# Expert gathers of two slots for 64 tokens, with the weighted sums in pairs on the two column halves of TensorE

## The reference

```python
q = (xb @ p['peer_wq']).reshape(PEER_CHUNK, PEER_HEADS, 2, PEER_KEY_HALF)
s = jnp.einsum('thcd,ckd->thck', q, p['peer_subkeys'])
sv, si = lax.top_k(s, PEER_TOPK)
...
gate = jax.nn.softmax(top_s, axis=-1)
u = jnp.take(p['peer_u'], eidx, axis=0)
v = jnp.take(p['peer_v'], eidx, axis=0)
act = jax.nn.gelu(jnp.einsum('ted,td->te', u, xb), approximate=False) * gate
return jnp.einsum('te,ted->td', act, v)
```

## Time and profile before

| what | value |
|---|---|
| times of 3 runs | 2964.49, 2954.89, 2937.0 us; median 2954.89 us |
| the profiled execution | 2938.93 us, of which the span from the first to the last instruction is 2936.8 us |
| mean granted TensorE clock | 0.88 of full speed |
| moved by DMA | 976.17 MB, of it 805.36 MB by the gathers |

### The profile page before, as it was taken

One profiled execution on the slowest core, in us unless ns is written; L12 is line 12 of the kernel. 1 busy time (PEld: TensorE's weight loads), 2 busy tenths in 40 slices (PEclk: granted clock), 3 DMA queues, 4 the chain that ended last, 5 costly groups with the idle time before them and its releaser, 6 DMA issues.

```text
span 2936.8 us, 25913 instructions
## 1 busy us (share of the span) xinstructions
PE 2216.8 (75%) x6672; PEld 1099.9 (37%) x6672; DVE 1858.5 (63%) x4486; ACT 1074.9 (37%) x2975; POOL 951.4 (32%) x868
## 2 busy tenths in 40 slices
PE   6997777769788878767768877777766787766765
PEld 1434433544444435323323323233453343432322
DVE  0134966884567758877865555453579575867775
ACT  2022444452345544333342233232235344433332
POOL 0001323333233323334343434330023333344553
PEclk8998888889898999888889989888988888888888
DMA  5455989988787799899999999995189879999997
GB/s 187 125 175 194 392 324 346 374 338 326 300 313 281 281 369 386 338 417 382 393 404 411 393 394 397 401 396 179 65 318 378 334 302 352 400 370 411 420 411 316
DMA packets 223768, 976.17 MB, mean 332 GB/s; under 512 B 18300, under 2 KB 71064, under 8 KB 125336
## 3 DMA queue, kind: packets, MB, share of 16 engines
q0 software_dynamic: 110592, 805.36, 68.2%
q1 hardware_dynamic: 113048, 169.32, 17.0%
HBM read 973.56 MB, written 1.05 MB: 332 GB/s over the span
## 4 chain that ended last, share of the span: by engine, by line
PE 36%; DMA 25%; DVE 22%; issue 9%; ACT 5%; POOL 2%; POOLq 0%; SPq 0%; DVEq 0%; ACTq 0%; PEldq 0%
DMA EXPERT<-in_peer_uv,FIX 21%; PE VS L853 13%; PE PA L722 10%; DVE EXPERT L1429 7%; PE PB L676 4%; DVE SCR L1081 3%; PE PB L842 2%; DVE ACC L1439 2%; DMA WT<-in_w_ada 2%; PE PA L750 2%; POOL EXPERT L598 2%; PE PB L790 1%; DMA WT<-in_w_in 1%; PE PA L798 1%; PE PA L738 1%
## 5 line engine op out<-in xcount | busy, mean ns | idle before, releaser
L853 PE MATMUL VS<-EXPERT,DIAG 128*128 128x512 f32 x2304 | 1137.2, 644 | 281.7 <-ACT DIAG L1036 271.2
L1429 DVE CUSTOM_DVE_ANT_0 EXPERT<-EXPERT,H 128x1024 f32<-128x1024 f32 x768 | 925.6, 1223 | 493.2 <-DMA EXPERT<-in_peer_uv,FIX 486.6
L598 POOL DMA_INDIRECT EXPERT<-in_peer_uv,FIX x768 | 900.0, 1172 | 988.0 <-PE VS L853 494.7
L853 PEld LDWEIGHTS VS<-EXPERT,DIAG 128*128 128x128 f32 x2304 | 458.0, 207 | 915.0 <-issue 532.0
L1029 ACT ACTIVATE GEL<-DOT 128x1 f32<-128x1 f32 x768 | 154.8, 202 | 1049.0 <-DVE DOT L1429 1047.5
L722 PE MATMUL PA<-WT,HT 128*128 128x512 f32 (+2 forms) x768 | 329.5, 584 | 51.0 <-ACT QTD L966 17.3
L590 POOL COPY FIX<-IDX 128x8 uint32 (+1 forms) x96 | 51.2, 533 | 966.8 <-PE VS L853 529.6
L1036 ACT ACTIVATE DIAG<-IDN,WEI 128x128 f32<-128x128 f32 x576 | 231.3, 402 | 126.1 <-PE VS L853 109.8
L1439 DVE SCALAR_TENSOR_TENSOR ACC<-EXPERT,WEI,ACC 128x1024 f32<-128x1024 f32 x192 | 245.9, 1281 | 2.2 <-ACT WEI L1031 1.8
L842 PE MATMUL PB<-HT,WT 128*128 128x128 f32 (+1 forms) x1280 | 200.5, 322 | 46.6 <-issue 46.6
L1031 ACT ACTIVATE WEI<-GEL,GATE 128x1 f32<-128x1 f32 x768 | 226.2, 295 | 24.9
(11 more groups left out here) (137 smaller groups left out, 1656.5 us busy)
## 6 DMA issues: line engine op xcount, KB each, us to landing
WT<-in_w_ada SPq DMA_DIRECT2D x96, 512.0 KB, 7.1
WT<-in_peer_wq SPq DMA_DIRECT2D x80, 512.0 KB, 9.4
WT<-in_w_in SPq DMA_DIRECT2D x56, 512.0 KB, 10.5
WT<-in_w_out SPq DMA_DIRECT2D x40, 512.0 KB, 4.8
EXPERT<-in_peer_uv,FIX POOLq DMA_INDIRECT x768, 10.5
WT<-in_w_in SPq DMA_DIRECT2D x16, 384.0 KB, 7.2
WT<-in_w_in SPq DMA_DIRECT2D x20, 288.0 KB, 6.8
WT<-in_mla_wk_up SPq DMA_DIRECT2D x5, 512.0 KB, 3.9
```

What stands on the lines that cost most here:

```text
L598: pool.indirect_dma_start(out=EXPERT[:, j, :], out_offset=None, in_=a["peer_uv"], in_offset=bass.IndirectOffsetOnAxis(ap=FIX[:, par, j:j + ...
L853: ins = nc.tensor.matmul(VSUM[n][:, :], DIAG[:, i, :], EXPERT[:, j, D + n * W:D + (n + 1) * W], start=first, stop=last_one)
L1429: nc.vector.tensor_tensor_reduce(out=EXPERT[:, j, 0:D], in0=EXPERT[:, j, 0:D], in1=H2[:, b % HB, :], scale=1.0, scalar=0.0, op0=ALU.mult, ...
```

## The change

A gather now brings, in one buffer of EXPERT, two slots for 64 tokens in place of one slot for 128: buffers with an even number carry tokens 0 to 63, with an odd number tokens 64 to 127, and in each the lower 64 partitions hold one slot of these tokens and the upper 64 partitions the next one. The bytes and the number of gathers are the same. What follows from it:

- `apply` on PE works on a pair of buffers. The stationary matrix of each is 128x64 (two scaled 64x64 identities on top of each other, TWO times WEI), so that the product sums the two slots and gives 64 output rows: those of the even buffer go to partitions 0 to 63 of VS0 and VS1, those of the odd one to partitions 64 to 127, which are the two column halves of the array. A pair has four products (eight MATMULs), a quad eight products (sixteen MATMULs) in place of six (twelve). PE does all slots; DVE's `apply` and the clearing of ACC are gone.
- DIAG is 128x64 with eight buffers (one for each of EXPERT's), made for every slot; it no longer waits for PE.
- POOL waits for PE alone.
- IDX and GATE are written with slots and tokens rearranged: four instructions of 64 partitions x 8 elements for each, IDX's on DVE, GATE's on ACT, which now waits for DVE's reciprocal. That reciprocal is moved ahead of the comparison with IOTA.
- H2 holds each half of the tokens twice (`back`: eight copies of 64x512 for a block in place of two of 128x512) and has two buffers in place of three; IDX and GATE keep three (`IB`). `back` of the second latent block of layer 0 is moved behind the search for that block and the modulation beside it.
- ACC shrinks to 512 columns, MROW moves into unused partitions of QTM, and `close` is rewritten: the gate's row is copied first, and multiplied with the bank.

```diff
-HB = 3
+HB = 2
+IB = 3
+G = P // 2
-BY_PE = 3
...
-        out += [("norm", l, g, t, 2), ("back", l, g, t)]
+        out += [("norm", l, g, t, 2)] + ([("back", l, g, t)] if t == ts[0] else [])
...
+    if s[0] in ("pick", "also") and s[3] == 1:
+        return [("close", b - IB) for b in blocks_of(s[1], s[2]) if b >= IB]
...
-    picks = mingle(picks[5:], modulation(1, 0, 4)) + [("mod", 1, 1)]
+    picks = mingle(picks[5:], modulation(1, 0, 4)) + [("mod", 1, 1), ("back", 0, LAT, 1)]
...
-        H2 = sb("H2", [P, HB, D])
+        H2 = sb("H2", [P, HB, 2, D])
-        DIAG = sb("DIAG", [P, BY_PE, P])
+        TWO = sb("TWO", [P, G])
+        DIAG = sb("DIAG", [P, RING, G])
...
-                    if j % 4 < BY_PE:
-                        wait(used_pe, (n * 2 - 2 + j // 4) * BY_PE + j % 4 + 1)
-                    else:
-                        wait(used_dve, n * 2 - 2 + j // 4 + 1)
+                    wait(used_pe, (n - 1) * UNIT + j + 1)
...
-            def apply(no, i, j, first=False, last_one=False):
-                pe.wait_ge(diag_ready, no + 1)
+            def apply(no, j, first=False, last_one=False):
+                pe.wait_ge(diag_ready, no + 2)
                 for n in range(2):
-                    ins = nc.tensor.matmul(VSUM[n][:, :], DIAG[:, i, :], EXPERT[:, j, D + n * W:D + (n + 1) * W],
-                                           start=first, stop=last_one)
-                ins.then_inc(used_pe, 1)
+                    for g in range(2):
+                        ins = nc.tensor.matmul(VSUM[n][g * G:(g + 1) * G, :], DIAG[:, j + g, :],
+                                               EXPERT[:, j + g, D + n * W:D + (n + 1) * W], start=first, stop=last_one)
+                        if n == 1:
+                            ins.then_inc(used_pe, 1)
...
                 nc.scalar.activation(TE[:, t, :], TS[:, t, :], ACT.Exp, bias=NT[:, t:t + 1],
                                      accum_out=TSUM[:, t:t + 1]).then_inc(topexp_ready, 1)
+                act.wait_ge(inverse_ready, tick("inverse"))
+                for g in range(2):
+                    mine = slice(g * G, (g + 1) * G)
+                    parted = TE[mine, t, :].rearrange("p (q s) -> p q s", s=2)
+                    for s in range(2):
+                        to = GATE[s * G:(s + 1) * G, b % IB, h * TOPK:(h + 1) * TOPK].rearrange("p (q g) -> p q g", g=2)
+                        ins = nc.scalar.activation(to[:, :, g], parted[:, :, s], ACT.Copy, scale=TINV[mine, t:t + 1])
+                link(ins)
...
-                if i < BY_PE:
-                    act.wait_ge(wei_ready, no + 1)
-                    if not isinstance(mine, int) or mine >= BY_PE:
-                        act.wait_ge(used_pe, mine - BY_PE + 1)
-                    nc.scalar.activation(DIAG[:, i, :], IDN[:, :], ACT.Copy, scale=WEI[:, one]).then_inc(diag_ready, 1)
+                act.wait_ge(wei_ready, no + 1)
+                nc.scalar.activation(DIAG[:, j, :], TWO[:, :], ACT.Copy, scale=WEI[:, one]).then_inc(diag_ready, 1)
...
-                    nc.vector.tensor_copy(H2[:, b % HB, half * W:(half + 1) * W], bank[:, :]).then_inc(emptied_a, 1)
+                    for g2 in range(2):
+                        for s in range(2):
+                            ins = nc.vector.tensor_copy(H2[s * G:(s + 1) * G, b % HB, g2, half * W:(half + 1) * W],
+                                                        bank[g2 * G:(g2 + 1) * G, :])
+                    ins.then_inc(emptied_a, 1)
...
-            def apply(no, quad, j):
-                dve.wait_ge(wei_ready, no + 1)
-                if not isinstance(quad, int) or quad > 0:
-                    dve.wait_ge(used_dve, quad)
-                nc.vector.scalar_tensor_tensor(out=ACC[:, :], in0=EXPERT[:, j, D:2 * D], scalar=WEI[:, BY_PE:BY_PE + 1],
-                                               in1=ACC[:, :], op0=ALU.mult, op1=ALU.add).then_inc(used_dve, 1)
```

94 lines of the change are left out of this document (44 added, 50 removed).

## The result

| | before | after |
|---|---|---|
| median of 20 runs | 2948.56 us | 2961.86 us |
| ratio, 95% interval | | 1.0046 [1.003, 1.0062] |
| profiled execution | 2938.93 us | 2955.78 us, span 2954.0 us |
| mean granted clock | 0.88 | 0.826 |

A forecast was written before the change was run, and what follows sets the result against it. DMA gathers were taken to bound the saturated stretches, with at most 158 us of DMA idle time to win elsewhere. A gain of 87 less 22 of costs gave 65 us less, forecast 2882 us, range 2825 to 2960.

The forecast's parts named there:

- the gain in the sum, 87 us: Open stretches, where DMA idles: 58 us in 410 to 1110, 24 in 2270 to 2570, 5 beside; bounds 66 and 158.
- the halves overlap: PE's sums: column halves work at once, so a quad's sixteen MATMULs take about 3.5 to 3.9 us.
- Rival 1: PE's column halves follow each other, 6.87 us a quad; whole kernel near 3070 us; chance 0.11.
- four fifths: PE's busy share in 410 to 1110 us, used to count 70 of 88 us of sums as time.
- 28 + 16 us: A third of PE's sums in the chain of the two open stretches, taken as the least gain.
- 0.92: Sign: DMA's share in what was 410 to 1110 us rises to near this, the stretch about 50 us shorter.
- 760 us: Sign: PE's sums busy for near this long in place of 1137.
- The 18 us of DVE's sums: DVE's sums held 2.6% of the chain in 410 to 1110 us, counted as sure gain when they go.
- the clock, 6 us: Less PE work may lower TensorE's granted clock, lengthening other PE work in the open stretches; 6 us, bounds 0 and 24.
- rivals 3 and 4: 3: path moves to gathers and copies, about 2925 us, 0.21 with another rival; 4: pairs starve saturated stretches, 100 us, 0.03.
- the small instructions: Added work around the search: H2 copies on DVE 8 us, IDX on DVE 4, gate copies on ACT 4.
- 22 us of costs: Sum of added H2, IDX and gate work and the lower clock; DIAG nothing; bounds 0 and about 120.

The follow-up runs named there:

- bype4: Kernel before, with all four slots of a quad summed on PE's full array, eight DIAG buffers, no DVE sum, `close` as changed; 0.9944 of before.
- bype4_gate: bype4 with the gate in four copies on ACT behind a wait for the reciprocal, which is moved ahead; 0.9967 of before.
- bype4_extras: bype4 with IDX in four instructions, GATE in four copies on ACT, and four 64x512 copies to H2 a block; 0.9994 of before.
- full_single: Changed kernel with zero-padded 128-column stationaries (no overlap of halves), four DIAG buffers, PE taking one buffer at a time; 1.0032 of before.
- single_warm: single plus one product of two zero columns behind each pair to hold up PE's clock; 0.9951 of before.
- single: Changed kernel, but PE takes one buffer at a time instead of a pair; halves can still overlap; 1.0007 of before.
- full_pair: Changed kernel with its pairs, but zero-padded 128-column stationaries, so halves can't overlap, and four DIAG buffers; 1.0193 of before.
- before_warm: Kernel before plus two zero products for each quad, making PE as busy as in bype4, DVE's sums kept; 1.0045 of before.
- warm: Changed kernel plus one product of two zero columns behind each pair, after its buffers are given back; 1.0024 of before.
- bype4_pair: bype4 with only the pair added: one wait for two diagonals, four products, both buffers given back together; 1.01 of before.
- bype4_h2two: bype4 with H2 in two buffers, IDX and GATE in three, and `back` of the second latent block moved; 0.9924 of before.

## Why the prediction was wrong

The step that failed is the gain in the sum, 87 us, and above all the worth of TensorE's saved time in it; the second is the pair, which the sum put at nothing. The runs can be put in a row from before to after, a step each (differences of ratios, each uncertain by about 0.3 to 0.4, so that the second and third can't be told from nothing and the fourth hardly):

| step | from, to | change |
|---|---|---|
| DVE's sums to PE, full array (with `close` and DIAG's buffers) | before, bype4 | -0.56% |
| gate on ACT | bype4, bype4_gate | +0.23% |
| IDX and H2 in smaller instructions | bype4_gate, bype4_extras | +0.27% |
| gathers' layout, four more copies | bype4_extras, full_single | +0.38% |
| halves at once, at a clock held by zero products | full_single, single_warm | -0.81% |
| the zero products go, the clock falls | single_warm, single | +0.56% |
| pair | single, after | +0.39% |
| sum | | +0.46% |

The sum comes out by construction, since the steps run from before to after; it confirms none of them.

- **Right: the halves overlap.** Sixteen MATMULs in 3.65 us, forecast 3.5 to 3.9, and 7.03 without it. Rival 1 is refuted in its mechanism. Its price was far off too: without overlap it came to 3070 us by my sum; full_pair, just that with the pair, measured 2993, and full_single 2950, beside 2937 for the kernel before on their chip. I had charged PE's added time at four fifths. Also right: no wait of POOL for DVE or of DIAG for PE, DIAG at 348 ns against an estimate of 350, a copy of half the partitions at 689 ns.
- **Wrong, the largest step: the gain of 87 us.** In the row of steps 0.56 + 0.81 = 1.4%, 40 us, is gained. I took PE's share of the chain (28 + 16 us) as a sure part and four fifths of the saved busy time as the likely one. But a share of the chain is no saving: when PE is sooner done, the gather and the search are next. Three runs show what PE's time is worth. before_warm adds products of 349 us and costs 13. From full_single to single PE's sums are busy for 441 us less, and 7 us are gained, if any. bype4 has 297 us more of PE's sums and takes 0.56% less time, with DVE's sums gone. DMA's share in the open stretch was to rise to 0.92 and stayed at 0.85, and PE's sums were to be busy for 760 us and took 877.5 at the lower clock. The 18 us of DVE's sums in that chain were read as a small term; with what goes with them they were the cheaper part to win (1.0% against before_warm).
- **Not settled: the clock, 6 us.** It did fall, from 0.88 to 0.826, and to 0.75 in the last stretch. What that costs is bounded only roughly: bringing it back to 0.880 (warm) gained 0.22%, 6 us, within the intervals, and holding it at 0.91 in single gained 0.56%, 16 us, both net of the zero products. Neither is outside my bounds of 0 and 24; whether 6 was too little is not shown.
- **Wrong: rivals 3 and 4, the pair, which stood in the sum with nothing.** It cost 0.39% or 11 us, and 46 us in bype4_pair, where the halves don't overlap. I named the pair's wait (2.48 us for the even buffer), and set it aside by the earlier trace rows, a steady stretch in which eight buffers hide it. The cost isn't there; after the change the steady distance is still 2.48 us near the end. It arises behind a search, when POOL has no buffer, the gathers in flight run out and the first buffer to come back decides when they go on. These pauses stand in the trace of before too (78 gaps of over 7 us between dot products); I read a stretch without one.
- **Not refuted: the small instructions.** 8 + 4 + 4 = 16 us forecast, 0.50% or 15 us measured. The two don't match as well as they look: bype4_extras has only two of the six added copies a block, so that the forecast for it would be about 11 us (an estimate, a third of the 8), and the measured value is uncertain by 0.3%. For the gate I had counted on 3 us of cover and not seen that its wait would expose the table load.
- **Not priced at all: the layout,** with the other four copies 0.38% or 11 us, if it isn't uncertainty. What in it costs stays open. The two H2 buffers and the moved `back` cost nothing (bype4_h2two).

In this row, then, 87 us were 40, and 22 us of costs were 0.50 + 0.38 + 0.56 + 0.39 = 1.83%, 54 us; the difference is the 13 us measured. That the order of several of these steps could be another, and their values with it, isn't tried out; the clock's and the pair's depend on what else stands (the pair cost 0.39% or 1.6%).

## What to carry to other kernels

A slot of a ring that is given back later is to be priced at the place where the ring stands still, right behind a pause of the consumer, not in the steady stretch where its depth hides it. A share of the chain of waits bounds nothing from below: before counting on a faster engine, give it more to do in an experiment, and nothing else. Here products of 349 us cost 13, which would have spoken against four fifths. When work is taken from TensorE, the granted clock of the work that stays can fall, and a part of the gain with it.

## What the runs showed of the hardware

- Float32 products of 128 rows by 64 columns on the two column halves overlap fully: sixteen MATMULs, each with a weight load, in 3.65 us against 7.03 on the full array. The Trainium skill ("TensorE: Matmul & The Clock Gate", Part 3) says that a weight load overlaps running products only where its row group differs. Here all loads have the same rows, and the trace doesn't agree: the 3.65 us are eight steps of 0.43 us and the end of the last MATMUL, half of the full array's, so no load stood in the open.
- The granted clock followed PE's work: 0.826 after, 0.866 in single, 0.880 before, 0.91 to 0.93 in single_warm, full_single and bype4. Added products of zeros made one kernel faster (single to single_warm, -0.56%) and another slower (before to before_warm, +0.45%). What decides between the two isn't shown.
- A table load that stood behind a wait instruction of its own did not run ahead of that wait, and one whose Gelu carried the wait did. It showed as 41.0 us of waits for the dot product in front of table loads after the change, and none before.
- A VectorE copy out of PSUM took 689 ns for 64 and for 128 partitions of 512 elements (the earlier trace rows and the groups above).
